# Attention gates projected inside the attention rounds, in units of 256 tokens

## The reference, cut to what matters

```python
aq, ak, av, az, mq, mk, mv, mo, mz, mi, mf = project(xn, w_in)      # the same for ctx
q = rope_2d(aq.reshape(B, T, ATT_HEADS, ATT_HEAD_DIM), tables)      # 8 heads of 64
k = rope_2d(ak.reshape(B, T, ATT_KV_HEADS, ATT_HEAD_DIM), tables)   # 2 key heads
att_x = window_ctx_attention(q, k, v, kc, vc, sink) * jax.nn.silu(az)
...
out_x = jnp.concatenate([att_x, m_x], axis=-1) @ w_out
x = x + gate_x * out_x
```

## Time and profile before

| | us |
|---|---|
| median of 3 runs | 4123.25 |
| lowest, highest | 4116.99, 4129.21 |
| the profiled execution, its own time | 4116.82 |
| its span in the trace | 4115.0 |
| TensorE busy | 3802.5 (92% of the span) |
| VectorE, ScalarE, GpSimd busy | 1779.8, 926.5, 609.4 |
| mean granted TensorE clock | 0.962 of full speed |

### The profile page before, as it was taken

The page is one execution under the profiler, slowest core; times in us unless marked ns, Lnnn a source line. Parts: engine busy times, 40 slices in busy tenths (PEclk is TensorE's granted clock), DMA queues, the critical chain, the costliest instruction groups (busy, mean ns, idle before and its releaser), DMA issues.

```text
span 4115.0 us, 47845 instructions
## 1 busy us (share of the span) xinstructions
PE 3802.5 (92%) x19086; PEld 2385.5 (58%) x19086; DVE 1779.8 (43%) x3880; ACT 926.5 (23%) x1755; POOL 609.4 (15%) x553
## 2 busy tenths in 40 slices
PE   6899979978999999999998998899899998899899
PEld 3478874855476444444444577766554557775454
DVE  3677761264443233344334635421451544521441
ACT  5123321131100300000016113211451311220441
POOL 3001210041000222222224002110001002211001
PEclk8999989989999999999999999999999999999999
DMA  6201112054354111111112113211000412221101
GB/s 235 74 14 31 30 52 65 31 166 157 116 176 152 41 51 41 41 45 48 41 36 107 57 41 83 62 55 41 36 17 10 158 32 77 67 65 41 37 26 41
DMA packets 215403, 277.79 MB, mean 68 GB/s; under 512 B 24301, under 2 KB 174024, under 8 KB 214288
## 3 DMA queue, kind: packets, MB, share of 16 engines
q1 hardware_dynamic: 201904, 206.17, 16.1%
q0 software_dynamic: 13280, 68.57, 4.4%
HBM read 239.89 MB, written 34.81 MB: 67 GB/s over the span
## 4 chain that ended last, share of the span: by engine, by line
PE 84%; DVE 8%; issue 3%; ACT 2%; DMA 1%; POOL 1%; POOLq 0%; DVEq 0%; SPq 0%; ACTq 0%
PE ps L3075 17%; PE ps L1035 17%; PE ps L2946 8%; PE ps L3959 6%; PE ps L1057 6%; PE ps L4240 4%; PE ps L2707 3%; PE ps L3910 2%; PE ps L4449 2%; PE ps L3143 1%; PE ps L4432 1%; PE ps L1083 1%; DVE big L4060 1%; PE ps L1732 1%; DMA big<-hs_scratch 1%
## 5 line engine op out<-in xcount | busy, mean ns | idle before, releaser
L3075 PE MATMUL ps<-big 128*128 128x512 f32 x1624 | 697.1, 592 | 0.0
L1035 PE MATMUL ps<-big 128*128 128x512 f32 (+1 forms) x1760 | 685.0, 550 | 2.9 <-DMA big<-hs_scratch 2.9
L1035 PEld LDWEIGHTS ps<-big 128*128 128x128 f32 x1760 | 335.5, 192 | 343.4 <-issue 334.1
L3075 PEld LDWEIGHTS ps<-big 128*128 128x128 f32 x1624 | 308.6, 190 | 388.4 <-issue 385.3
L2946 PE MATMUL ps<-big 128*128 128x512 f32 (+1 forms) x896 | 359.3, 562 | 3.0 <-DVE big L4567 2.0
L2946 PEld LDWEIGHTS ps<-big 128*128 128x128 f32 x896 | 169.6, 190 | 187.7 <-issue 180.8
L3268 DVE SCALAR_TENSOR_TENSOR big<-ps,big 128x512 f32<-128x512 f32 x212 | 159.1, 751 | 242.7 <-PE ps L3075 208.7
L3959 PE MATMUL ps<-big 128*128 128x256 f32 x1152 | 252.3, 380 | 6.5 <-DVE big L4138 3.3
L1057 PE MATMUL ps<-big 128*128 128x256 f32 (+1 forms) x1344 | 235.9, 339 | 10.2 <-DVE big L2197 10.2
L3959 PEld LDWEIGHTS ps<-big 128*128 128x128 f32 x1152 | 218.0, 190 | 36.8 <-issue 7.1
L1057 PEld LDWEIGHTS ps<-big 128*128 128x128 f32 x1344 | 213.7, 196 | 31.6 <-DVE big L2197 10.3
(11 more groups left out here) (490 smaller groups left out, 5304.9 us busy)
## 6 DMA issues: line engine op xcount, KB each, us to landing
big<-in_w_mlp SPq DMA_DIRECT2D x32, 1024.0 KB, 5.4
big<-in_w_in SPq DMA_DIRECT2D x29, 1024.0 KB, 5.2
big<-in_w_mod SPq DMA_DIRECT2D x24, 1024.0 KB, 5.4
big<-in_w_ada SPq DMA_DIRECT2D x24, 1024.0 KB, 6.6
big<-us_scratch SPq DMA_DIRECT2D x72, 256.0 KB, 4.4
hs_scratch<-big POOLq DMA_DIRECT2D x3, 5120.0 KB, 14.9
big<-c_dft SPq DMA_DIRECT2D x12, 1024.0 KB, 5.8
xs_scratch<-big POOLq DMA_DIRECT2D x16, 640.0 KB, 3.7
```

The costliest lines, as they stand in the source:

```text
L1035: t = e.matmul(b[:, 0:n], wv[:, k, 128 * m:128 * m + 128], K.hT[:, k, t0:t0 + n], start=(k == 0), stop=(k == 7))
L3075: t = e.matmul(z, w[:, k, c], y, start=(first and k == 0), stop=(k == nk - 1), skip_group_check=not first)
```

## The change

`AttProj` no longer projects the gates; its weight loads stay where they were. Each round of `Attention` gets gate units instead. A unit is one tile of 128 features over 256 tokens (8 matmuls, 16 records). Round 0 has four (all of tokens 0 to 255), each later round two (behind the steps h = 0 and h = 2), until all 5 pairs of blocks (layer 0) or 4 (layer 1) are done: 20 and 16 units. A unit's result goes to a PSUM bank that has nothing else to do at that step: 7, 2, 3, 7 for h = 0 to 3. ScalarE copies it raw into `m.cat` behind the step's exponentials, and after every even round one Silu runs over 4 x 256 elements in place. `finish` waits for that Silu before it multiplies.

Because `hT` must now live through the rounds, its region can't hold `m.S[1]`, whose eight tiles go to four places: the region of the rope tables, free memory, and the ring slot that the value weights had. So the second tile of `OutProj`'s weights and those behind it are held on SP's queue until the last transposes that read `m.S[1]`. The stream is fetched whole, by one transfer, once the last gate unit is done; `RestoreX` goes. The fetch of the final gain waits for the end of layer 1's attention.

```diff
 class Finish(Stage):
     def __init__(self, K, sums, g):
-        super().__init__(K, "finish", "finish")
+        super().__init__(K, "finish", "finish", "at1")
     def fetch(self, e):
         L = self.lane("final_gain_in")
+        self.begin(e)
         e.dma_start(self.gb, self.g.partition_broadcast(128)).then_inc(...)
 class OutProj(Stage):
     def sync(self, e):
         for j in range(0, 8, 2):
+            if j == 2 and self.held is not None:
+                e.wait_ge(*self.at(*self.held))
             self.K.W.put_cols(e, self.w, 128 * j, 256)
 class AttMem:
-        second = Arena(K.big, K.M0 + 15360, K.M0 + 20480)
-        self.S = [B1.get(8, 640), second.get(8, 640)]
+        self.slot = slot
+        first = B1.get(8, 640)
         self.PT = [[B1.get(512) for _ in range(2)] for _ in range(2)]
+        ring = Arena(K.big, 5900 + 2048 * slot, 5900 + 2048 * slot + 2048)
+        tables = Arena(K.big, H1.at - 2 * T, H1.hi)
+        self.S = [[first[:, c, :] for c in range(8)],
+                  [tables.get(640) for _ in range(4)] + [B1.get(640)] + [ring.get(640) for _ in range(3)]]
 class AttProj(Proj):
     def tensor(self, e):
+        assert K.W.uses % 4 == m.slot
         self.tm(e, P, "v", 128, range(10), Banks(K, (4, 5, 6, 7)))
-        self.cm(e, P, "z", 4, Banks(K, (0, 1, 2, 3)), self.blks)
     def scalar(self, e):
-        for j in range(4):
-            for t0, n in self.blks:
-                u = (self.tag, "z", j, t0)
-                e.wait_ge(*self.at("mm", u))
-                e.activation(m.cat[:, j, t0:t0 + n], self.bank(u)[:, 0:n], ACT.Silu).then_inc(...)
 class Attention(Stage):
+    def gates(self, i, h):
+        if i == 0:
+            return [(0, h)]
+        p = (i + 1) // 2
+        return [(p, 2 * (1 - i % 2) + h // 2)] if h % 2 == 0 and 2 * p < len(self.blocks) else []
     def order(self, steps):
...
                 if i < nb:
                     steps.exps(i, h)
+                for p, j in self.gates(i, h):
+                    steps.gate(i, h, p, j)
...
+            if i % 2 == 0 and i < nb:
+                steps.silu(i // 2)
     def gpsimd(self, e):
-        self.begin(e)
-        e.dma_start(K.XT[:, 0:4, :], K.xs[:, 0:4, :]).then_inc(X.sem, X.up(by=16))
+        n = 128 * len(self.blocks)
+        e.wait_ge(*self.at("mm", self.key("gate", len(self.blocks) // 2 - 1, 3)))
+        e.dma_start(K.XT[:, :, 0:n], K.xs[:, :, 0:n]).then_inc(X.sem, X.up(("x back", f"two{self.l}"), by=16))
 class AttTensor(AttSteps):
+    def gate(self, i, h, p, j):
+        e, P, K = self.e, self.P, self.s.K
+        if p == 0 and j % 2 == 0:
+            self.weights.append(K.W.use(e, 256))
+        used, wv = self.weights[j // 2]
+        u, bank = self.key("gate", p, j), (self.R, self.N[0], self.N[1], self.R)[h]
+        b = bank.open(e, u)
+        for k in range(8):
+            t = e.matmul(b[:, 0:256], wv[:, k, 128 * (j % 2):128 * (j % 2) + 128], K.hT[:, k, 256 * p:256 * p + 256],
+                         start=(k == 0), stop=(k == 7))
+        t.then_inc(P.sem, P.up(("mm", u), used))
 class AttScalar(AttSteps):
+    def gate(self, i, h, p, j):
+        e, S, u = self.e, self.S, self.key("gate", p, j)
+        e.wait_ge(*self.at("mm", u))
+        e.activation(self.m.cat[:, j, 256 * p:256 * p + 256], self.s.bank(u)[:, 0:256], ACT.Copy).then_inc(
+            S.sem, S.up(("free", u, 0), self.key("gated", p)))
+    def silu(self, p):
+        e, S, z = self.e, self.S, self.m.cat[:, :, 256 * p:256 * p + 256]
+        e.wait_ge(*self.at(*self.key("gated", p)))
+        e.activation(z, z, ACT.Silu).then_inc(S.sem, S.up(self.key("silu", p)))
 class AttVector(AttSteps):
     def finish(self, i):
...
+        e.wait_ge(*self.at(*self.key("silu", n // 2)))
 def plan(K):
-        yield RestoreX(K, "restore", f"two{l}", f"at{l}", 4, TT if l == 0 else T)
...
         yield OutProj(K, f"two{l}", A["p_out"][l], (md[:, 16:24, 0], md[:, 16:24, 1]), blks, f"at{l}", sums, post,
-                      "ml1" if l == 0 else None)
+                      "ml1" if l == 0 else None, ("mm", (f"at{l}", "turned", 9 - 2 * l, 1 + 2 * l, 1)))
```

More of the change, by code:

```diff
@@ L2915, with __init__ @@
 class OutProj(Stage):
-    def __init__(self, K, tag, w, gates, blks, after, sums, post, away=None):
+    def __init__(self, K, tag, w, gates, blks, after, sums, post, away=None, held=None):
         super().__init__(K, "out_proj", tag, after)
+        self.held = held
         self.w, self.gates, self.blks, self.sums, self.post, self.away = w, gates, blks, sums, post, away
@@ L4169, with __init__ @@
 class AttMem:
-    def __init__(self, K, hT):
+    def __init__(self, K, hT, slot):
         H1, B1, CX = Arena(K.big, K.total - 10240, K.total), Arena(K.big, K.M0 + 20480, K.total - 10240), K.columns()
@@ L4263, in scalar @@
             e.activation(m.vtm[:, t, :], self.bank(u)[:, 0:nn], ACT.Copy).then_inc(S.sem, S.up(("free", u, 0)))
-        for j in range(4):
-            for t0, n in self.blks:
-                u = (self.tag, "z", j, t0)
-                e.wait_ge(*self.at("mm", u))
-                e.activation(m.cat[:, j, t0:t0 + n], self.bank(u)[:, 0:n], ACT.Silu).then_inc(
-                    S.sem, S.up(("free", u, 0)))
     def vector(self, e):
@@ L4368, in exps @@
     def exps(self, i, h):
+        pass
+    def gate(self, i, h, p, j):
+        pass
+    def silu(self, p):
         pass
@@ L4394, in __init__ @@
         self.O, self.R = Banks(K, (stage.ids["O"],)), Banks(K, (stage.ids["R"],))
+        self.weights = []
+    def gate(self, i, h, p, j):
[9 more added lines that the diff above has]
+        t.then_inc(P.sem, P.up(("mm", u), used))
     def q(self, i, g, h):
@@ L4432, in turn @@
                 t = e.transpose(b[:, 128 * h:128 * h + 128],
-                                self.m.S[i % 2][:, 2 * h + g, 128 * place:128 * place + 128], self.ident)
+                                self.m.S[i % 2][2 * h + g][:, 128 * place:128 * place + 128], self.ident)
             t.then_inc(P.sem, P.up(("mm", u)))
@@ L4485, in exps @@
         for g in range(2):
-            x, c = m.S[i % 2][:, 2 * h + g, self.s.first(n):self.s.end(n)], 2 * h + g
+            x, c = m.S[i % 2][2 * h + g][:, self.s.first(n):self.s.end(n)], 2 * h + g
             e.activation(x, x, ACT.Exp, bias=m.nm[:, c:c + 1], accum_out=m.sm[:, c:c + 1]).then_inc(
@@ L4520, in scores @@
                         e.tensor_tensor_reduce(
-                            S[:, c, 512:640], self.s.bank(u)[:, 128 * x:128 * x + 128], m.wm[:, 512:640], 64 ** -0.5,
+                            S[c][:, 512:640], self.s.bank(u)[:, 128 * x:128 * x + 128], m.wm[:, 512:640], 64 ** -0.5,
                             m.snk[:, c:c + 1], ALU.add, ALU.max, m.m0[:, c:c + 1]).then_inc(
@@ L4531, in scores @@
                 e.wait_ge(*self.at(*self.key("exp", i - 1, h, g)))
-            e.tensor_tensor_reduce(S[:, c, c0:512], self.s.bank(u)[:, c0:512], m.wm[:, c0:512], 64 ** -0.5,
+            e.tensor_tensor_reduce(S[c][:, c0:512], self.s.bank(u)[:, c0:512], m.wm[:, c0:512], 64 ** -0.5,
                                    (m.m0 if n < 7 else m.snk)[:, c:c + 1], ALU.add, ALU.max, m.mx[:, c:c + 1]).then_inc(
@@ L4801, in plan @@
         yield Close(K, f"ml out{l}")
-        m = AttMem(K, m.hT)
+        m = AttMem(K, m.hT, l)
         yield AttProj(K, l, m, f"ml out{l}")
```

## The result

Four runs of the changed kernel gave a median of 4053.68 us (4052.65 to 4056.97); four of the kernel before, 4124.95 (4116.99 to 4129.21). The ratio is 0.983, with an interval of 0.981 to 0.985: faster by 1.7%. The forecast was 4058, in a range of 4047 to 4082. The profiled execution took 4056.97, of which its span is 4055.2; before it was 4115.0, so 59.8 us less where the sum had 59.3.

The account below looks back on a forecast made before the run. TensorE was taken as the bound, with the gates' projection on its path and holes in the rounds. 62.4 - 1.3 - 1.8 = 59.3 us off 4116.8 gave 4057.5, stated as 4058, range 4047 to 4082.

Parts of the forecast that it names:

- What bounds the kernel: TensorE carries 84% of the chain; gates' projection, 125.6 us, is on the path; rounds have holes of about 2.12 us.
- What a unit costs: One gate unit of 16 records on TensorE costs 3.48 us, the 36 units 125 us: work moved, not reduced.
- The rounds: Attention with units: full round 23.3 us, round 0 18.5; layer 0 gains 30.6 us, layer 1 31.8, together 62.4.
- The clock: TensorE in the rounds: slow stretches of 1.6 us follow the hole and go with it, leaving a clock of 1.00.
- ScalarE: In the rounds: 15.2 us of work in 23.3, Silu over 1024 elements about 1.0, table loads 1.28 each, mostly covered.
- The uncovered ones: Exp table loads in layer 0's round 9 and layer 1's round 7, without unit as cover: 0 to 2.6 us, 1.3 taken.
- PSUM, DMA and queues: Banks, held `OutProj` tiles (5.2 us each) and the whole stream fetch (about 21 us) cost nothing.
- The sum: Whole kernel: 62.4 less 1.3 for loads and 1.8 for edges gives 59.3 us gained.
- the clock still falls: Rival: rounds 1 to 6 of both layers keep 1.6 us each, 19 us more, 4077; chance 0.10.
- a full round gains nothing: Rival: the unit lies behind the wait, the softmax chain binds, 125 us only change place, 4117; chance 0.03.
- ScalarE as a link: Rival: TensorE waits for a table load and raw copy in 14 rounds with two units, 23 us, 4081; chance 0.09.
- The slower case: Rival: TensorE at half clock for much of the gated rounds, 105 us longer at 0.79, 4163; chance 0.04.

Follow-up runs that it names:

- Experiment 1: Changed kernel with all gate units issued ahead of round 0, the rest of the change kept: 4121.27 us, ratio 1.0009 to the kernel before.
- experiment 2: Changed kernel with only the second units of rounds 1 and later issued ahead of round 0: 4055.64 us, ratio 0.9839 to the kernel before.
- experiment 3: Changed kernel with the first unit of rounds 1 and later behind the scores of step 1, so behind the wait: 4102.62 us, ratio 0.9956 to the kernel before.
- experiment 4: Kernel before plus four matmuls nobody reads, ahead of the wait in rounds 1 to 6 of both layers: 4102.08 us, ratio 0.9945 to the kernel before.
- experiment 5: Changed kernel with each unit evicted by its own Silu, no raw copies: 4072.74 us, ratio 0.988 to the kernel before.
- experiment 7: Changed kernel with the stream fetched only when attention has ended in each layer: 4061.63 us, ratio 0.9849 to the kernel before.
- 6: Changed kernel with tile 0 of the output projection's weights held on SP's queue as well: 4069.67 us, ratio 0.9866 to the kernel before.

## Why the prediction was right, step by step

**What bounds the kernel.** Right: gates on the path, holes in the rounds. Experiment 1 moves the units out of the rounds and the time is that of before.

**What a unit costs.** 3.48 us was the estimate from the mLSTM. Ahead of the rounds it was 3.47 (experiment 1, 69.31 for 20) and 3.48 (experiment 2); in a round 3.55 and 3.65 from its start to the next score. In a full round, 23.46 - (18.54 - 2.13) = 7.05 for two, 3.53 each: the edge is about 0.05, the value I took. In round 0 it is more, 0.1 a unit: 18.92 instead of 18.5.

**The rounds.** Forecast and measured, in us: round 0 18.5 and 18.92; round 1 21.3 and 21.15; full rounds 23.3 and 23.46, with the edges 23.4; round 7 22.3 and 22.34; round 8 18.5 and 18.53; round 9 9.0 and 9.13; the flush 6.4 and 6.3. Layer 0 from its first score: 212.7 and 1.0 for 20 edges make 213.7, measured 213.65. Layer 1 from its first score: 182.8 and 0.8 make 183.6, measured 183.74. The first scores start 0.41 us behind the values' last product, where 0.6 had been allowed.

**The clock.** Right, and the causal step, "it follows the hole", is the one that the experiments carried. The hole put back gives the slow stretch in every full round (experiment 3, with the same matmuls in a round as the changed kernel); the hole filled with idle work takes it away (experiment 4). "It follows the hole each time" holds one way only. Every slow stretch in the full rounds has a hole ahead of it, but not every hole is followed by one: round 6 of layer 0 before, experiment 3's round 1 and two of the full rounds shown in experiment 1 have a hole of 2.0 to 2.1 us and a clock of 1.00. What decides between such rounds stays open. The rule quoted from the Trainium skill's "TensorE: Matmul & The Clock Gate", section "Part 4: PE-mode transpose", that transposes don't engage the full clock, did not decide here: the rounds with 40 transposes stand at 1.00.

**ScalarE.** The Silu over 1024 elements took 1.06 us, where 1.0 was estimated. There are 11 and 9 table loads of 1.28, as counted. The uncovered ones were the term that was wrong in size: 1.3 us was taken for round 9 and layer 1's round 7, and they cost nothing. TensorE's waits of round 9 are 0.45, 1.08 and 0.25 us, where they were 0.44, 1.08 and 0.25 before:

```profile
3040.17 0.70 PE L4453 MATMUL ps<-big 64*128 64x256 f32 x4 [0.45 <-DVE big L4576]
3044.62 0.70 PE L4453 MATMUL ps<-big 64*128 64x256 f32 x4 [1.08 <-DVE big L4576]
3048.48 1.19 PE L4465 MATMUL ps<-big 128*128 128x128 f32 x8 [0.25 <-ACT big L4512]
```

The first two are VectorE's reading of the scores, the third a copy of ScalarE's. The exponentials of step 0 began 3.2 us into the round instead of 2.3, and none of these waits grew by it. Of the two parts of a switch of which the Trainium skill's "ScalarE: Activation LUTs", section "What ACT_TABLE_LOAD costs", speaks (1.28 and 1.38 us of drain), the runs show the 1.28 and no second one: in experiment 5's rows above the load starts at 2952.78, right behind the copies, and the exponential at 2954.08, 1.30 later. With 54 loads more in that experiment the two attentions grew by 16.7.

**PSUM, DMA and queues.** All free, as forecast. The whole stream is one transfer of 5120 KB and took 16.4 us instead of the 21 allowed; VectorE's first sum in `OutProj` waits for TensorE (7.45 us), not for the stream. `OutProj`'s held weights took 8.0 us a tile by the median, where the prediction had 5.2 from the earlier trace rows. The stream is not the reason: its packets had stopped before the three tiles were issued at 3049.70, and in layer 1, where the stream had landed 15 us earlier, they took 9.0, with the fetch of the final gain beside them. The three go out together and share the DMA engines; the tile of 5.2 went out by itself, and even beside the 2560 KB of the stream. 8.0 stayed within the 13.9 us that tile 0 gives.

```profile
big<-xs_scratch POOLq DMA_DIRECT2D x1, 5120.0 KB, 16.4
big<-in_p_out SPq DMA_DIRECT2D x3, 1024.0 KB, 8.0
```

By stretch, ahead of the three tiles and while they land (the last number of a row is GB/s):

```profile
3049.00:3050.00 1.00, 1.00 (x8) 0.62 (x8) 0.23 (x2) 0.83 (x2) 0.00 (x0) 1.00 0.00 0
3053.00:3060.00 7.00, 6.58 (x16) 3.02 (x17) 0.22 (x1) 0.00 (x0) 0.00 (x0) 1.00 1.09 352
```

The head of `OutProj` on TensorE and VectorE:

```profile
3053.42 26.85 PE L2949 MATMUL ps<-big 128*128 128x512 f32 x62 [1.02 <-DVE big L4612]
3060.66 0.75 DVE L2970 SCALAR_TENSOR_TENSOR big<-ps,big 128x512 f32<-128x512 f32 x1 [7.45 <-PE ps L2949]
```

**The sum.** 59.3 forecast; the two layers gave 60.5. The sum is near for good reasons: its two largest errors are 1.3 for loads that cost nothing and 2 x 0.4 for round 0. That the traces differ by 59.8 is nearer still, and partly chance: 2.7 us lost ahead of layer 0's values, 2.0 won outside of the two attentions. The absolute time, 4058, owes something to luck as well. It was taken from one short execution of before; from the median of before it would have been 4064, and the median of after came out at 4053.68.

**Where the gain came from.** By each round's length less its units (3.65 each in round 0, 3.53 elsewhere), in both layers together:

- Round 0 was 11.75 us and is 18.92 - 14.6 = 4.3 without its units: 7.4 less, twice, 14.8.
- Round 1 was 20.25 and 20.19, and is 21.15 - 7.05 = 14.1: 12.2 less. In it VectorE was behind from round 0, and the clock had fallen.
- The ten full rounds were 20.1 to 20.5 where slow, 18.5 in round 6 of layer 0, and are 23.46 - 7.05 = 16.4 each. About 36 less, of which ten holes of 2.13 are 21.3 and nine slow stretches of 1.6 are 14.4.
- Rounds 7 and 8 give 1.2. The 36 units cost 8 x 3.65 + 28 x 3.53 = 128.0 us where the projection took 125.6: 2.4 back.

That makes 61.8, of which 60.5 were measured. Of the rest 0.8 is the 0.41 us that TensorE now waits ahead of the first score of each layer, 0.5 lies in rounding and in the stages' ends. The second units, 14 of the 36, gave none of it (experiment 2).

**The rivals.** That the clock still falls, and that a full round gains nothing, is true with the unit one place later: a full round of experiment 3 takes 27.34 us, and one of before with two units added 20.1 + 7.05 = 27.2. Its median of 4102.62 is below that of before since round 0 keeps its gain and round 1 two thirds of its own (23.28 instead of 20.25 + 7.05, where the changed kernel has 21.15). ScalarE as a link is real at one Silu per unit (4072.74), and not with raw copies. The slower case did not arise; nothing here had a clock under 0.92 in a full round.

**Left open.** The 0.2 us by which a second unit is dearer in a round than ahead of it (14 of them, 2.8 us) could be had by experiment 2's order. Its two layers are 1.8 us shorter from the values to `OutProj`, but the medians don't separate it from the changed kernel. What the medians' 71.3 us have beyond the traces' 59.8 was not traced. The order of tiles beyond the first was not tried.

## What to carry to other kernels

Work moved into a hole is worth the hole and the slow stretch behind it, if there is one, and only if it stands ahead of the wait in the engine's own order: one place later, the same 14 units cost 45.6 us of span. Look for the instruction behind the hole that runs long (here 1.97 us for 1.09 of transposes): it tells that the hole costs more than its length. When an activation of another table is moved in between exponentials, copy raw and apply it once for several units, where the engine idles anyway; one at every unit cost 16.7 us here.

## What the runs showed of the hardware

- Work that nobody reads made a kernel faster. With 1.7 us of products in a hole of 2.12, the full rounds went from 20.1 to 18.54 us, and the kernel gained 17 us by the medians. A hole of 0.39 us (0.74 in one round) left the granted clock at 1.00 in all ten full rounds. One of 2.12 us or more was followed in 27 of 30 full rounds by a stretch that cost 1.6 to 1.75 us (9 of 10 before, 8 in experiment 1, 10 in experiment 3). Two rounds with the same hole and the same work differ in this, within one kernel.
- The same code ahead of the attention ended at different times in different kernels' profiles. The values of layer 0 began at these times, in us: 2817.35 in experiment 2, 2818.65 before, 2820.56 in experiment 1, 2821.33 after, 2824.16 in experiment 5, 2824.45 in 3, 2825.53 in 7, 2826.31 in 6 and 2827.30 in 4. The granted clock of the first 500 us goes with it at the ends, 0.95 and 0.96 in the two earliest and 0.91 in the latest, experiment 4; between them it is 0.93 to 0.95. So two spans can differ by up to 10 us by the code ahead of the attention alone, while the length of a stage repeats closely (213.65 and 213.66 for layer 0's attention in two kernels).
- Transfers in flight together share the rate. The 5120 KB of the stream landed in 16.4 us alone, at 441 GB/s in round 9, and in 19.1 in experiment 7, where it set out beside the end of the three tiles of `OutProj`'s weights. Three tiles of 1024 KB issued together landed in 8.0 us (the median), with nothing else under way, at 352 GB/s; a single one, issued just ahead of 2560 KB of the stream, took 5.2.
